# First layer's attention with its values made turned: norm factor at the residual addition and, inverted, in the gated half; ring slot released behind the last values

## The reference, cut to what matters

```python
def rms_norm(x, gain):
    x32 = x.astype(jnp.float32)
    y = x32 * lax.rsqrt(jnp.mean(x32 * x32, axis=-1, keepdims=True) + EPS)
    return y.astype(x.dtype) * gain
...
    def attend(qb):                                   # in gqa_group
        s = jnp.einsum('bkgqd,bksd->bkgqs', qb, kh).astype(jnp.float32)
        p = jax.nn.softmax(s, axis=-1).astype(vh.dtype)
        return jnp.einsum('bkgqs,bksd->bkgqd', p, vh)
...
    return rms_norm(o, out_gain)                      # o: (B, T, 512)
...
    return o * jax.nn.silu(g)                         # end of gla_group
...
    mixed = jnp.concatenate([o_gla, o_att], axis=-1)  # in first_block
    h = h + mixed @ w_out[l]
    h = h + hier_moe(rms_norm(h, norm2_gain[l]), ...)
```

## Time and profile before

| | |
|---|---|
| median of 3 runs | 1505.77 us (1503.89 to 1508.84) |
| the profiled execution | 1507.1 us, span 1505.3 us |
| TensorE busy | 1262.7 us, 84% |
| VectorE, ScalarE, GpSimd busy | 430.9, 282.4, 49.8 us |
| mean granted TensorE clock | 0.942 of 2.4 GHz |
| DMA | 493.24 MB, mean 328 GB/s; 428 to 430 GB/s while the experts stream |
| TensorE first at an expert (line 1060) | 159.12 us |

### The profile page before, as it was taken

How to read it: one execution, slowest core, us unless ns; L and a number is a source line. 1 busy time by engine, 2 the same in 40 slices (tenths; PEclk the granted TensorE clock), 3 DMA queues, 4 the chain that set the end, 5 groups by cost and what they waited for, 6 DMA issues and landing times.

```text
span 1505.3 us, 32827 instructions
## 1 busy us (share of the span) xinstructions
PE 1262.7 (84%) x14582; PEld 927.5 (62%) x14582; DVE 430.9 (29%) x892; ACT 282.4 (19%) x687; POOL 49.8 (3%) x90
## 2 busy tenths in 40 slices
PE   9999977678767777786777787776899999999998
PEld 5565855556555556565555565564545486888854
DVE  1553322121121221221221211212215213466644
ACT  3433211111111110210111211111212212211100
POOL 4101000000000000000000000000100000000000
PEclk9999999988899997988999889989999999999999
DMA  9529899999999999999999999999973342454420
GB/s 342 191 85 353 361 429 428 428 428 428 428 428 429 427 430 427 430 427 430 428 429 428 429 428 429 428 429 428 407 267 112 112 157 81 142 194 168 168 84 28
DMA packets 78597, 493.24 MB, mean 328 GB/s; under 512 B 4856, under 2 KB 28624, under 8 KB 53856
## 3 DMA queue, kind: packets, MB, share of 16 engines
q1 hardware_dynamic: 76560, 486.69, 78.8%
q0 software_dynamic: 1600, 5.17, 1.2%
q10 hardware_dynamic: 400, 0.86, 0.1%
HBM read 491.65 MB, written 1.05 MB: 327 GB/s over the span
## 4 chain that ended last, share of the span: by engine, by line
DMA 54%; PE 43%; issue 1%; DVE 1%; POOL 1%; ACT 0%; SPq 0%; DVEq 0%; POOLq 0%
DMA ring<-in_w_gate_dram 46%; PE bank L1366 7%; DMA ring<-in_w_up_dram 7%; PE bank L1060 6%; PE bank L1161 6%; PE bank L695 5%; PE bank L1401 4%; PE bank L781 3%; PE bank L1331 2%; PE bank L719 2%; DMA ring<-in_w_in_dram 1%; PE bank L675 1%; PE bank L1089 1%; PE bank L901 1%; PE bank L1037 1%
## 5 line engine op out<-in xcount | busy, mean ns | idle before, releaser
L1060 PE MATMUL bank<-ring,big 128*32 128x128 f32 x8192 | 304.3, 310 | 175.4 <-DMA ring<-in_w_gate_dram 113.9
L1060 PEld LDWEIGHTS bank<-ring,big 128*32 128x32 f32 x8192 | 262.3, 125 | 226.9 <-DMA ring<-in_w_gate_dram 85.4
L1089 PE MATMUL bank<-ring,big 128*32 128x256 f32 x2048 | 130.3, 395 | 45.0 <-DMA ring<-in_w_down_dram 44.4
L2097 DVE TENSOR_TENSOR big<-big,bank 128x128 f32<-128x128 f32 x64 | 24.2, 377 | 471.0 <-PE bank L1060 471.0
L1608 ACT ACTIVATE big<-bank 32x256 f32<-32x256 f32 x128 | 47.8, 373 | 444.5 <-PE bank L1089 442.9
L2108 DVE COPY big<-bank 32x256 f32<-32x256 f32 x128 | 54.1, 423 | 226.2 <-PE bank L1089 224.2
L1089 PEld LDWEIGHTS bank<-ring,big 128*32 128x32 f32 x2048 | 66.5, 112 | 84.8 <-issue 32.3
L1161 PE MATMUL bank<-ring,xT 128*128 128x512 f32 x192 | 86.5, 597 | 0.3 <-ACT xT L1460 0.3
L1075 PEld LDWEIGHTS bank<-aux,c 128*128 128x128 f32 x512 | 67.3, 205 | 15.6 <-issue 15.6
L1075 PE MATMUL bank<-aux,c 128*128 x512 | 76.2, 295 | 0.0
L1037 PE MATMUL bank<-big,xn 128*128 128x128 f32 x544 | 72.7, 289 | 0.2 <-DVE big L2045 0.2
(11 more groups left out here) (382 smaller groups left out, 1430.1 us busy)
## 6 DMA issues: line engine op xcount, KB each, us to landing
ring<-in_w_gate_dram SPq DMA_DIRECT2D x64, 2048.0 KB, 25.8
ring<-in_w_up_dram SPq DMA_DIRECT2D x64, 2048.0 KB, 27.2
ring<-in_w_down_dram SPq DMA_DIRECT2D x63, 2048.0 KB, 27.1
ring<-in_w_gate_up_dram SPq DMA_DIRECT2D x22, 1024.0 KB, 6.7
ring<-in_w_in_dram SPq DMA_DIRECT2D x14, 1024.0 KB, 17.2
ring<-in_w_down_dram SPq DMA_DIRECT2D x12, 1024.0 KB, 7.0
ring<-in_w_in_dram SPq DMA_DIRECT2D x3, 2048.0 KB, 27.0
ring<-in_w_out_dram SPq DMA_DIRECT2D x2, 2048.0 KB, 16.9
```

The source lines that it names most:

```text
L1060: i = pe.matmul(dst[TOK * j:TOK * (j + 1), 0:P], xg[:, k, TOK * q:TOK * (q + 1)], w[:, k, j * P:(j + 1) * P], start=(k == 0), stop=(k == K ...
L1089: i = pe.matmul(bank[6 + q % 2][TOK * m:TOK * (m + 1), 0:SEQ], hT[:, q % 2, TOK * k:TOK * (k + 1)], w[:, k, SEQ * m:SEQ * (m + 1)], start= ...
```

## The change

- **Values turned.** `gqa_values` now takes two groups at once. The values are the weights (64 columns) and the turned probabilities move (128 columns); the output stands turned in bank 5, two heads on top of each other. `probsT` has two buffers. It runs at n = 3, 5, 7, 9.
- **Softmax's division** moves ahead of the turn: VectorE's `gqa_scale(n)` multiplies the probabilities by the inverse of their sums, and the turn waits for it.
- **The attention's half is not transposed** for the output product. `att_gained` multiplies bank 5 by the gain, one factor per partition (`att_col`), straight into the operand.
- **The norm factor** cannot be applied there, since tokens lie in columns. ScalarE squares bank 5, TensorE sums over partitions with a column of ones (`att_sums`), VectorE copies the sums into `stat`, GpSimd makes the factor. The residual addition multiplies the whole product by it; the gated half is multiplied by its inverse in `mix_tile`, so that the factor cancels there.
- **Order.** The loop has two projection matmuls ahead of the turn and one behind it. The output product is split into an attention part and a gated part of four matmuls each.
- **Slot 5** is loaded behind the last values and the GLA output; the loads behind it wait for the second mixed tile. The gain comes in one small load on ScalarE's queue, the broadcast load on GpSimd's is gone.

```diff
@@ sync
                 if PRE_UNITS + u - RING == SCRATCH:
                     sp.wait_ge(*at("gla_o", TT))
                     sp.wait_ge(*at("gqa_pv", len(GQA_PAIRS) * TT))
-                    sp.wait_ge(*at("mix_n", TT))
...
                 if PRE_UNITS + u - RING == SCRATCH:
+                    sp.wait_ge(*at("mix_n", TT))
                     resident(aux[:, 0:4 * D], 0, 4, D, "cvw_in")
@@ gpsimd
-            load(att_gain, t_in["att_out_gain"][0:1, :].to_broadcast([P, 512]), "attgain_in")
...
-            rstd_tile("att", 0, 2, 512)
             for t in range(TT):
                 rstd("gla", GLA_H, GLA_DV, 8 + GLA_H * t, t + 1)
-            rstd_tile("att", 1, 2, 512)
+                rstd_tile("att", t, 2, 512)
@@ tensor
             def gqa_turn(n):
-                pe.wait_ge(*at("gqa_exp", n + 1))
+                pe.wait_ge(*at("gqa_scaled", n + 1))
...
+            def gqa_values(pair):
+                pe.wait_ge(*at("gqa_PT", 2 * pair + 2))
+                if pair == 2:
                     pe.wait_ge(*at("att_o", 1))
+                for j in range(2):
                     for k in range(TT):
+                        for g in (2 * pair, 2 * pair + 1):
+                            h = GQA_PAIRS[g % 4][j]
+                            o = 64 * (h % 2)
+                            i = pe.matmul(bank[5][o:o + HD, h // 2 * P:(h // 2 + 1) * P],
+                                          proj[:, k, C_AV + (h // 4) * HD:C_AV + (h // 4 + 1) * HD],
+                                          probsT[g % 2][:, (2 * j + k) * P:(2 * j + k + 1) * P], start=(k == 0), stop=(k == TT - 1))
+                i.then_inc(S("gqa_pv"), 2)
+            def att_sums(t):
...
+                for c in range(4):
+                    i = pe.matmul(bank[3][:, t:t + 1], att_sq[t][:, c * P:(c + 1) * P], C1("ones", 0, 1), start=(c == 0), stop=(c == 3))
+                i.then_inc(S("att_sum"), 1)
...
             for n in range(10):
                 if n < 8 and n % 2 == 0:
                     gqa_scores(n)
-                if n >= 2:
-                    gqa_values(n - 2)
+                if n >= 3 and n % 2 == 1:
+                    gqa_values((n - 3) // 2)
+                if n < 9:
+                    project(2)
                 if 1 <= n < 9:
                     gqa_turn(n - 1)
-                if n < 9:
-                    project(3 if n < 8 else 2)
+                if n < 8:
+                    project(1)
...
                 if n == 8:
-                    pe.wait_ge(*at("mix_n", 1))
-                    transposes("mix", mix, 0, 2)
+                    att_sums(0)
...
+            out_part(0, 0, "att")
+            att_sums(1)
+            gla_transposes(0)
+            out_part(1, 0, "att")
+            out_part(0, 0, "gla")
+            gla_transposes(1)
+            out_part(1, 0, "gla")
+            out_part(0, 1, "att")
+            out_part(0, 1, "gla")
             pe.wait_ge(*at("out_ev0", 2))
             transposes("n2", x, 0, 4)
+            out_part(1, 1, "att")
+            out_part(1, 1, "gla")
@@ scalar
+            act.dma_start(gain_rows[7 * KD:7 * KD + 4, :], t_in["att_out_gain"][0].rearrange("(k p) -> k p", p=P)
+                          ).then_inc(S("colgain_in"), 16)
             squares("n1", x, 0, mix, lambda t: act.wait_ge(*at(f"x_in{t}", 16)))
...
             def att_squares(t):
+                act.wait_ge(*at("gqa_pv", 4 * (t + 1)))
+                A(att_sq[t], bank[5][:, :], ACT.Square).then_inc(S("att_sq"), 1)
@@ vector
+            def gqa_scale(n):
+                c = 8 * (n // 4) + GQA_PAIRS[n % 4][0]
+                dve.wait_ge(*at("gqa_exp", n + 1))
+                link(V.reciprocal(ersum[:, c:c + 3:2], esum[:, c:c + 3:2]))
+                for j in range(2):
+                    p = probs[:, n % 2, j * SEQ:(j + 1) * SEQ]
+                    i = V.tensor_scalar(p, p, ersum[:, c + 2 * j:c + 2 * j + 1], None, ALU.mult)
+                i.then_inc(S("gqa_scaled"), 1)
...
+            def att_gained(t):
+                dve.wait_ge(*at("att_sq", t + 1))
+                V.tensor_tensor(att_oT[t], bank[5][:, :].rearrange("p (k s) -> p k s", k=4),
+                                att_col.unsqueeze(2).to_broadcast([P, 4, P]), ALU.mult).then_inc(S("att_o"), 1)
...
             def mix_tile(t):
                 dve.wait_ge(*at("att_rstd", t + 1))
-                V.scalar_tensor_tensor(mix[:, t, 512:1024], o_att[:, t, :], stat[:, 2 + t:3 + t], att_gain, ALU.mult, ALU.mult)
+                link(V.reciprocal(att_inv[:, t:t + 1], stat[:, 2 + t:3 + t]))
                 dve.wait_ge(*at("gg_silu", t + 1))
-                V.tensor_tensor(mix[:, t, 0:512], o_gla[:, t, :], gla_sg[:, t, :], ALU.mult).then_inc(S("mix_n"), 1)
+                V.scalar_tensor_tensor(mix[:, t, 0:512], o_gla[:, t, :], att_inv[:, t:t + 1], gla_sg[:, t, :], ALU.mult, ALU.mult
+                                       ).then_inc(S("mix_n"), 1)
...
             gla_mask_scores(1)
             gqa_max(3)
+            gqa_scale(2)
             gqa_PT(2)
+            gqa_scale(3)
             in_evac(3)
             gqa_max(4)
             gqa_PT(3)
             gla_mask_scores(2)
             gla_mask_scores(3)
             gqa_max(5)
+            gqa_scale(4)
             gqa_PT(4)
+            gqa_scale(5)
             gla_states(0)
-            gqa_output(0)
             gqa_max(6)
+            att_gained(0)
             gqa_PT(5)
             gla_states(1)
             gqa_max(7)
+            gqa_scale(6)
             gqa_PT(6)
+            gqa_scale(7)
...
-                V.tensor_tensor(xs, xs, bank[(2 * u + t) % 4][:, :], ALU.add).then_inc(S(f"{name}_ev{t}"), 1)
+                V.scalar_tensor_tensor(xs, bank[(2 * u + t) % 4][:, :], stat[:, 2 + t:3 + t], xs, ALU.mult, ALU.add
+                                       ).then_inc(S(f"{name}_ev{t}"), 1)
```

More of the change, by code:

```diff
@@ L168, in build @@
                     base += n
-        for signal in ("sc", "nm", "exp", "ptp", "PT", "pv"):
+        for signal in ("sc", "nm", "exp", "scaled", "ptp", "PT", "pv"):
             for stage, base in (("gqa", 0), ("moba", 8), ("cross", 14)):
@@ L330, in build @@
         mem_junk = aux[:, 1024:3072].rearrange("p (t d) -> p t d", t=TT)
+        att_sq = [mix[:, 0, 0:512], mem_junk[:, 1, 0:512]]
+        att_inv = stat[:, 118:120]
         memT = c2[:, :].rearrange("p (k s) -> p k s", k=KD)
@@ L807, in _ @@
             i.then_inc(S("zT_tp"), 1)
-            pe.wait_ge(*at("colgain_in", 96))
-            pe.transpose(bank[7][:, 0:7 * KD], gain_rows, ident[0:7 * KD, 0:7 * KD]).then_inc(S("colgain_tp"), 1)
+            pe.wait_ge(*at("colgain_in", 112))
+            pe.transpose(bank[7][:, 0:7 * KD + 4], gain_rows, ident[0:7 * KD + 4, 0:7 * KD + 4]).then_inc(S("colgain_tp"), 1)
             for t in range(TT):
@@ new lines, in att_sums, with gla_transposes @@
+            def att_sums(t):
+                pe.wait_ge(*at("att_sq", t + 1))
+                if t == 0:
+                    pe.wait_ge(*at("gqa_exp", 8))
+                else:
+                    pe.wait_ge(*at("att_ss", 1))
+                for c in range(4):
+                    i = pe.matmul(bank[3][:, t:t + 1], att_sq[t][:, c * P:(c + 1) * P], C1("ones", 0, 1), start=(c == 0), stop=(c == 3))
+                i.then_inc(S("att_sum"), 1)
+            def gla_transposes(t):
+                pe.wait_ge(*at("mix_n", t + 1))
+                if t == 0:
+                    pe.wait_ge(*at("gla_sq", 4))
+                else:
+                    pe.wait_ge(*at("att_o", 2))
+                for k in range(4):
+                    i = pe.transpose(bank[6 - 2 * t + k // 2][:, (k % 2) * P:(k % 2 + 1) * P], mix[:, t, k * P:(k + 1) * P], ident)
+                i.then_inc(S("mix_tp"), 1)
@@ new lines, in out_part @@
+            def out_part(u, t, part):
+                w = slot(OUT_G[u]).rearrange("p (k c) -> p k c", k=KD)
+                pe.wait_ge(*at(f"w1_in{OUT_G[u] % RING}", 32))
+                if part == "att":
+                    pe.wait_ge(*at("att_o", t + 1))
+                else:
+                    wait_T("mix", t)
+                for k in (range(4, KD) if part == "att" else range(4)):
+                    a = att_oT[t][:, k - 4, :] if part == "att" else xT[:, k, t * P:(t + 1) * P]
+                    i = pe.matmul(bank[product_bank("out", u, t)][:, :], a, w[:, k, :], start=(k == 4), stop=(k == 3))
+                if part == "gla":
+                    i.then_inc(S("out_mm"), 1)
@@ L1547, in _ @@
                 gqa_exp(n)
+            att_squares(0)
             in_evac(4)
@@ L1558, in _ @@
             gla_copies(1)
-            evac_T("mix", tiles=(0,), b0=(2, 4))
             silu_gate(1)
             att_squares(1)
-            evac_T("mix", tiles=(1,), b0=(2, 4))
+            mix_evac(0)
+            mix_evac(1)
             for t in range(TT):
@@ L1896, in gqa_max, with att_total, mix_evac @@
                                 AX.X, ALU.max, negate=True).then_inc(S("gqa_nm"), 1)
```

(29 more changed lines are left out.)

35 lines of the change are left out of this document (10 added, 25 removed).

## The result

The changed kernel takes 1512.69 us (median of 9 runs, 1508.23 to 1515.10), the one before 1505.77 (9 runs): ratio 1.0035, 95% interval 1.002 to 1.005, that is 5.3 us (3.0 to 7.5). The ratio rests on all runs; the two medians by themselves lie 6.9 us apart. The changed kernel is slower, but the interval takes in 1.003, the line that the prediction drew between same and slower. The larger chance had gone to slower; 1512.5 was forecast.

The account below looks back on a forecast made before the run. TensorE's way to the first expert was taken to bound the kernel. Work -1.5, stalls +4.8 and clock +3.4 us on 1507.1 gave 1513.8, less 1.3 for the median: 1512.5 us, range 1507 to 1516.5.

Parts of the forecast that it names:

- What bounds the kernel: Ahead of the expert stream: TensorE's way to the first expert sets the time; a DMA gap swallows the slot 5 change.
- Work, -1.5 us: TensorE's work: values -2.3 us, half the transposes -0.9, new sums of squares +1.7, output products unchanged.
- The Trainium skill's rule on row groups: Values' column halves: by the rule nothing overlaps; the forecast followed a measured row instead, 0.064 us a record.
- Rival 3: Values groups: column halves do not overlap, 1.76 us a group instead of 1.02, +3.0 us, 1515.5; chance 0.06.
- The stalls, +4.8 us: TensorE waits for VectorE at first chunk products (1.05 us), second chunk products (2.2) and first output (1.55).
- The clock, +3.4 us: TensorE's clock falls to 1.2 GHz after stalls; two falls counted, each losing about 1.7 us of work.
- The sum: Whole kernel: 1507.1 + 3.3 + 3.4 = 1513.8 us profiled; median 1.3 lower, so 1512.5; chance of this forecast 0.50.
- Number 1: Stalls come, but the clock holds or falls only where a stall hides it: +3.3 us, 1509.1; chance 0.28.
- Number 4: A second order of waits (late probability copies, first turn, bare weight loads in sums): 0.5 to 2 us more, 1514; chance 0.08.
- Number 2: No stall decides, VectorE or the order being faster than reckoned: only -1.5 us of work is left, 1504.3; chance 0.08.

Follow-up runs that it names:

- e6: The changed kernel with the expert load into slot 5 again behind the second gated tile: 1509.60 us, ratio 1.0028 to the kernel before.
- e11: The changed kernel with VectorE's list in the new order and the slot 5 load again behind the second gated tile: 1504.22 us, ratio 0.9987.
- e9: The changed kernel with VectorE's list in the new order and each group of sums of squares done twice: 1505.68 us, ratio 0.9998.
- the version with all three moved: The changed kernel with VectorE's maskings 2 and 3, states 0 and states 1 each moved ahead of a turn's copy: 1503.86 us, ratio 0.9986.
- e0: The changed kernel itself run again, nothing altered: 1510.31 us, ratio 1.0035 to the kernel before.
- e8: The changed kernel with all values matmuls of one column half done before those of the other: 1511.89 us, ratio 1.0034.
- e10: The changed kernel with VectorE's maskings and states 1 moved ahead, states 0 left, so only the 2.4 us wait stays: 1507.53 us, ratio 1.0013.
- e1: The changed kernel with TensorE's loop back in the old order, turn first, then the projection matmuls: 1507.23 us, ratio 1.0010.
- e7: The kernel before with only the new order, two projection matmuls ahead of each turn and one behind: 1513.58 us, ratio 1.0053.

## Why the prediction was right

- **What bounds the kernel.** Right. TensorE's way to the first expert is what moves; the DMA gap ahead of it swallowed the slot's change (e6, e11), and the 1.7 us of work added in e9 lengthened the way by 1.7.
- **Work, -1.5 us.** Right, -1.4 us: the way of the version with all three moved is 91.13 us, that of the kernel before 93.82, of which 1.3 are a fall of the clock (lines 1022 to 1037 took 5.46 us, and 4.16 in e0). A wait of 0.2 us ahead of the first turn, taken as 0, is in it, so the work alone is -1.6. Values 1.02 us a group, sums 0.84, as priced.
- **The Trainium skill's rule on row groups.** The Trainium skill, "TensorE: Matmul & The Clock Gate", Part 3, The mechanism, says that a weight load overlaps running matmuls only when its row group differs. These tiles all use all rows, so by that rule the order of the column halves would make no difference. The trace disagrees: 0.064 us a record in alternation, 0.094 with the halves apart (e8). Rival 3 is out.
- **The stalls, +4.8 us.** The places, their order and their releasers were right; the sizes were all too small. The prediction counts from start to start, and so counted they are 1.27, 2.49 and 1.77 us where it had 1.05, 2.2 and 1.55 (the view, which begins at the end of a record, gives 1.20, 2.42 and 1.60). Together that is 5.5, not 4.8. Most of the 0.2 to 0.3 us at each place is the signal behind a turn. I had 0.44 + 0.04 us from the turn's start to the copy's; it is 0.63 or 0.64 (83.47 to 84.10, 89.99 to 90.63). The rows of before had it: 90.00 to 90.64. The 0.44 are start to start, and the record of the last transpose ends later, 0.60 us after the turn's start. That is 0.16 us a place. The rest is mainly the way back: 0.11 and 0.15 us from the end of VectorE's work to TensorE's start at the first two places (86.02 to 86.13, 93.72 to 93.87), where I had 0.04.
- **The clock, +3.4 us.** That a stall can bring the clock down was right; the count, and which stall, were half wrong. I had one fall each behind the stalls of 2.2 and of 1.55 us. Only the first brings them, in four executions of five, and in the profiled one for twice as long; the second never did. A fall of ordinary length cost 1.5 us of the way in e10 and 1.6 in e6 (98.28 us against 96.65 in e0), the long one 3.3, so that over the five profiles it is 1.6 us on average. The step that failed is reading a rule from one row: the fall behind 1.74 us at 30.36 came in two of the 13 profiles, whose idle times there are 0.87 to 2.26 us. What decides between a fall and none stays open.
- **The sum.** +6.7 was forecast. By the parts measured it is -1.4 + 5.5 + 1.6, or 5.7; the ratio says 5.3 (3.0 to 7.5). Two errors stood against each other, 0.7 too little for the stalls and 1.8 too much for the clock. That the median of the first nine runs fell on the forecast to 0.2 us is luck in the last two microseconds: the next seven had 1510.31.
- **Rivals.** Number 1 (stalls, the clock holds: 1509.1) is what e0's profile shows, an execution of 1509.19 us, and the truth lies between it and the forecast. Number 4 had the first turn right, at 0.2 us. Number 2 fell with the first trace; it is what the change becomes once VectorE's list is moved.

## What to carry to other kernels

Where engines run lists written by hand, moving work from behind a step to ahead of it also takes that step's cover away; before doing so, add up what the other engine does between that step's signal and the next thing waited for, and move ahead of the step whatever does not depend on it. Three moves in VectorE's list turned 1.0035 into 0.9986 without touching TensorE. Do not price a fall of the clock from one execution; profile several. Read the signal's delay from the start of the producing group to the start of the consumer, not from its neighbour's start.

## What the runs showed of the hardware

- The same wait of 2.42 us brought the granted clock to 1.2 GHz in four executions and not in a fifth, and in one of the four for 6.8 us instead of 3.4. Waits of 1.2 and 1.6 us brought it down in none of six, waits of 1.7 us in neither of two (e1, e7). Near 30 us idle times of 1.74 and 2.03 us did, and one of 2.26 us did not.
- Eight records with one column moving and full-size weights take 0.84 us (e9), as eight with 64 columns do.
- Records of 128 columns on 128*64 tiles take 0.064 us each with the two column halves in turn and 0.094 with one half after the other (e8); at full width they take 0.11 (four transposes in 0.44).
- VectorE starts on four transposes 0.63 or 0.64 us after their start, though TensorE's next instruction starts after 0.44.
